# High products ahead of low ones within a slice, and a final norm that is transposed in the last pair, scaled per token at the end

## The chip, the cores and the metric

The kernel runs on one core of a Trainium2 chip. The metric is device time in microseconds for one call. TensorE multiplies (its clock has two levels here, 1.2 and 2.4 GHz; the profile gives the granted share of 2.4), VectorE and ScalarE do elementwise work, GpSimd and SyncE issue transfers. Each engine works through its own instructions in order and waits on semaphores.

## What is computed

One inference step of a two-layer diffusion backbone on 128 context tokens and 128 latent tokens, all float32:

```python
def rms_norm(x, g):
    y = x * rsqrt(mean(x * x, axis=-1) + 1e-6)
    return y * g

for l in range(2):
    h = rms_norm(x, g_attn[l]) * (1 + scale1) + shift1      # modulation: silu(c) @ w_ada + b_ada
    proj = h @ w_in[l]                                      # 2048 -> 3584
    mix = concat(conv_module(...), global_attention(...), windowed_attention(...))
    x = x + gate1 * (mix @ w_out[l])                        # 2048 -> 2048
    h2 = rms_norm(x, g_mlp[l]) * (1 + scale2) + shift2
    x = x + gate2 * (square(relu(h2 @ w_mlp1[l])) @ w_mlp2[l])   # 2048 -> 8192 -> 2048
y = rms_norm(x, g_final)                                    # for both token groups
```

## The kernel before

The residual stream `xT` lies transposed in SBUF: 16 tiles of 128 channels, each with 256 token columns (128 context, 128 latent, `S` = 2 groups). Every weight matrix is cut into pairs of 512 output columns by 2048 rows; `walk` lists the pairs of a layer in order for all engines: in1, in2, in3, out, then four chunks of up and down. There are 43 pairs a layer, 86 in all. The pair of the last four output tiles is written apart from its loop and is called with `last` true.

A product in float32 is made of reduced-precision parts. ScalarE rounds a weight tile to `hi` (`split_hi`, L622), VectorE subtracts it from the raw weights to give `lo` (`split_lo`, L808). The activations are split too and lie side by side: columns 0 to 255 the high part, 256 to 511 the low part. Of the four partial products three are kept: `hi` times all 512 columns (L466), and `lo` times the 256 high ones, added onto columns 256 to 511 of the same bank (L468). ScalarE and VectorE then add both halves of the bank.

TensorE's loop is `pair` (from L447). For each half g of a pair (two banks, j = 0 and 1) it goes through four slices h of four k tiles; a slice waits once for its `lo` and, except in a fresh stage, once for its activations, and for each k it issues, for j = 0 and then j = 1, the high product and the low product. The last product of a slice increments `half_used`, which frees the slice's weight buffers. Weights pass through four `raw` buffers, loaded by SyncE, and four `hi` and `lo` buffers; `split_hi` number o of a pair waits until slice o - 4 is used. In ScalarE's and VectorE's `pair` the splits o = 4g+3 to 4g+6 stand ahead of the drains of half g, so ScalarE works in this order: four splits, the copy of two banks (L667), two squares of the new residual tiles (L678).

After the down pairs the residual is complete. VectorE has added up the squares per channel row in `ssq` (L888). Then comes the final norm, in order: TensorE sums the squares per token (`norm_stats`, L386), ScalarE takes the root (L796), VectorE the reciprocal `tok_rstd` (L1072), TensorE spreads it over all partitions into bank 7 (L390), VectorE multiplies each of 32 tiles by gain and spread value into `yT` (L1076), TensorE transposes them by fours (L612), ScalarE drains each bank into `xtok` (L800), and SyncE stores each drained 128x512 piece (L355), eight stores of 256 KB with rows of 2 KB.

Of the kernel before, what the change touches and what calls it, by code (L numbers as in the profile page):

```python
# [96 lines left out]
def build(nc, t):  # L97
# [77 lines left out]
    yT = place("yT", [P, KT, TOK], f32, act2_at)  # L175
# [50 lines left out]
    out_turned, out_drained, yT_ready = sem("out_turned"), sem("out_drained"), sem("yT_ready")  # L226
# [80 lines left out]
    with block:  # L307
# [3 lines left out]
        def _(sp):  # L311
# [40 lines left out]
            for b in range(8):  # L352
                s, q = b % 2, b // 2
                sp.wait_ge(out_drained, b + 1)
                sp.dma_start(t["y"][s].rearrange("a q d -> (a q) d")[:, q * 512:(q + 1) * 512],  # L355
                             xtok[:, s, q * 512:(q + 1) * 512]).then_inc(y_stored, 16)
            sp.wait_ge(y_stored, 8 * 16)
# [23 lines left out]
        def _(pe):  # L381
            def norm_stats(q):


                for s in range(S):
                    mm = pe.matmul(pb[7][:, s:s + 1], ssq[:, s * P:(s + 1) * P], ones[:, 0:1], start=True, stop=True)  # L386
                mm.then_inc(stat_ready, 1)
                pe.wait_ge(tok_rstd_ready, q + 1)
                for s in range(S):
                    mm = pe.matmul(pb[7][:, TOK + s * P:TOK + (s + 1) * P],  # L390
                                   tok_rstd[:, s:s + 1].to_broadcast([P, P]), ident, start=True, stop=True)
                mm.then_inc(rstd_spread, 1)

# [52 lines left out]
            for l in range(DEPTH):  # L446
                def pair(kind, n, i, c, a, last, l=l):  # L447
                    acts = act2 if kind in ("out", "down") else hs
                    for g in range(2):
# [4 lines left out]
                        for h in range(4):  # L454
                            pe.wait_ge(lo_ready, 8 * n + 4 * g + h + 1)
                            if kind == "down":
                                pe.wait_ge(act2_ready, hidden_base(l, c) + 4 * (h + 1))
                            elif kind != "out" and not fresh:
                                pe.wait_ge(hs_ready, (2 * l + (kind == "up")) * NORM_STEPS + 8 * (h + 1))
                            for k in range(4):  # L460
                                if fresh:
                                    pe.wait_ge(hs_ready, (2 * l + (kind == "up")) * NORM_STEPS + 8 * h + 2 * (k + 1))
                                for j in range(2):
                                    k_ = 4 * h + k
                                    bank = pb[2 * g + j]
                                    pe.matmul(bank[:, :], hi[:, h, k, j * P:(j + 1) * P], acts[:, k_, :],  # L466
                                              start=(k_ == 0), stop=False)
                                    mm = pe.matmul(bank[:, TOK:2 * TOK], lo[:, h, k, j * P:(j + 1) * P],  # L468
                                                   acts[:, k_, 0:TOK], start=False, stop=(k_ == KT - 1))
                            mm.then_inc(half_used, 1)  # L470
                            if a is not None and h == 2:
                                for u in range(2):
                                    ada_unit(*vector_of(kind, i, a, c), a, 4 * quarter(kind, i, a) + 2 * g + u)
                            if kind == "in3" and h % 2 == 1:
                                qk_norms(l, 4 * (i - IN2) + 2 * g + h // 2)
                    if a is not None and quarter(kind, i, a) == 3:
                        vl, vm = vector_of(kind, i, a, c)
                        ada_turn(vl * VECTORS + vm)

# [126 lines left out]
            norm_stats(2 * DEPTH)  # L606
            for b in range(8):
                s, q = b % 2, b // 2
# [8 lines left out]
        def _(act):  # L617
# [33 lines left out]
            for l in range(DEPTH):  # L651
                def pair(kind, n, i, c, a, last, l=l):
                    for g in range(2):
                        if kind == "in3":
                            qk_norms(l, 4 * (i - IN2) + 2 * g)
                        for o in range(4 * g + 3, 4 * g + 7):
                            if not (last and o >= 8):
                                split_hi(n, o)
                        if kind == "in3":
# [9 lines left out]
                        for j in range(2):  # L669
# [4 lines left out]
                            elif kind in ("out", "down"):  # L674
# [4 lines left out]
                                               ACT.Square).then_inc(sq_ready, 1)  # L679

# [113 lines left out]

            act.wait_ge(stat_ready, 2 * DEPTH + 1)
            act.activation(tok_std[:, :], pb[7][:, 0:S], ACT.Sqrt, bias=eps[:, :], scale=1.0 / D).then_inc(std_ready, 1)  # L796
            for b in range(8):
                s, q = b % 2, b // 2
                act.wait_ge(out_turned, b + 1)
                act.activation(xtok[:, s, q * 512:(q + 1) * 512], pb[b % 4][:, :], ACT.Copy).then_inc(out_drained, 1)  # L800
# [3 lines left out]
        def _(dve):  # L804
# [342 lines left out]
```

## Time and profile before

| | us |
|---|---|
| median of 3 runs | 2440.06 (2438.89 to 2440.91) |
| profiled execution, its own time | 2436.85 |
| its span, first to last instruction | 2435.2 |
| mean granted TensorE clock | 0.975 |
| TensorE busy, matmul | 2295.0 (94%) |
| TensorE busy, weight loads | 1826.7 (75%) |
| VectorE busy | 1518.7 (62%) |
| ScalarE busy | 1064.2 (44%) |
| last high-low products | to 2416.2 |
| final norm, transposes and stores | 2419.74 to 2435.2 |

The profile is one execution; it names engine, line, operation and tile of each group of instructions. Matmuls are pipelined: the recorded duration of a product is longer than the distance from one start to the next, and the distance is what a stream costs. A weight load overlaps the product ahead of it.

### The profile page before, as it was taken

What the parts mean: (1) busy time and instruction counts of PE and PEld (TensorE: products, weight loads), DVE (VectorE), ACT (ScalarE), POOL (GpSimd) and SP (SyncE); (2) the same over time, 40 slices, a digit from 0 to 9 for tenths busy, and PEclk for the clock granted to TensorE, in tenths of its full rate; (3) what the DMA queues carried; (4) which work ended last, traced back from release to release, by engine and by line L of the source; (5) the groups of instructions that cost most, each with busy time, mean ns of one, the idle gap of its engine ahead of it and who ended that gap; (6) DMA issues with size and microseconds to landing.
All of it is one profiled execution on the core that took longest, in us unless ns stands there. A gap on an engine that the chain in (4) does not pass through costs nothing.

```text
span 2435.2 us, 36896 instructions
## 1 busy us (share of the span) xinstructions
PE 2295.0 (94%) x13206; PEld 1826.7 (75%) x13206; DVE 1518.7 (62%) x2606; ACT 1064.2 (44%) x1663; POOL 101.6 (4%) x196
## 2 busy tenths in 40 slices
PE   5699879989999999999998997798999999999998
PEld 1277657767887887887786775586788888888886
DVE  0457775575665665565566678767566666666665
ACT  1343334454443443444444342455444545445443
POOL 2000000000000000000000000000000000000000
PEclk9699989999999999999999999999999999999999
DMA  9888645969579669768855885255956555555652
GB/s 386 331 332 300 243 180 211 320 242 324 182 244 319 231 198 314 254 196 294 295 183 204 301 318 214 97 187 189 313 198 196 176 193 186 182 194 176 193 188 87
DMA packets 390556, 570.29 MB, mean 234 GB/s; under 512 B 9604, under 2 KB 364472, under 8 KB 365624
## 3 DMA queue, kind: packets, MB, share of 16 engines
q1 hardware_dynamic: 360504, 365.51, 46.5%
q0 software_dynamic: 27648, 201.34, 20.5%
q10 hardware_dynamic: 2304, 2.10, 0.2%
q8 instruction: 65, 1.06, 0.2%
q14 instruction: 35, 0.29, 0.0%
HBM read 565.76 MB, written 3.15 MB: 234 GB/s over the span
## 4 chain that ended last, share of the span: by engine, by line
PE 86%; DVE 7%; DMA 4%; ACT 2%; issue 1%; POOL 0%; DVEq 0%; ACTq 0%; POOLq 0%
PE bank L466 52%; PE bank L468 26%; PE bank L403 6%; DMA ada<-in_w_ada 4%; DVE hs L1051 1%; DVE ybuf L1043 1%; DVE qrs L938 1%; DVE yconv L901 1%; DVE lo L808 1%; PE bank L483 0%; ACT prob L759 0%; DVE yT L1076 0%; PE bank L421 0%; PE bank L390 0%; PE bank L511 0%
## 5 line engine op out<-in xcount | busy, mean ns | idle before, releaser
L466 PE MATMUL bank<-hs,hi 128*128 128x512 f32 x2944 | 1067.6, 406 | 18.6 <-DVE hs L1051 9.9
L808 DVE TENSOR_TENSOR lo<-raw,hi 128x1024 fp32r<-128x1024 f32 x685 | 816.6, 1222 | 402.2 <-ACT hi L622 401.4
L622 ACT ACTIVATE hi<-raw 128x1024 fp32r<-128x1024 f32 x685 | 706.3, 1054 | 502.7 <-PE bank L468 497.4
L466 PE MATMUL bank<-act,hi 128*128 128x512 f32 x2560 | 908.0, 400 | 5.4 <-DVE act L989 5.4
L468 PE MATMUL bank<-hs,lo 128*128 128x256 f32 x2944 | 830.5, 282 | 0.0
L466 PEld LDWEIGHTS bank<-hs,hi 128*128 128x128 f32 x2944 | 557.9, 189 | 220.4 <-issue 56.4
L468 PE MATMUL bank<-act,lo 128*128 128x256 f32 x2560 | 719.3, 281 | 0.0
L466 PEld LDWEIGHTS bank<-act,hi 128*128 128x128 f32 x2560 | 482.4, 188 | 131.5 <-issue 6.7
L468 PEld LDWEIGHTS bank<-hs,lo 128*128 128x128 f32 x2944 | 560.9, 191 | 2.5 <-issue 2.5
L468 PEld LDWEIGHTS bank<-act,lo 128*128 128x128 f32 x2560 | 484.8, 189 | 0.0
L667 ACT ACTIVATE tmp<-bank 128x256 f32<-128x256 f32 x344 | 113.5, 382 | 443.9 <-PE bank L468 443.9
L863 DVE TENSOR_TENSOR tsum<-bank,tmp 128x256 f32<-128x256 f32 x288 | 121.0, 420 | 237.6 <-ACT tmp L667 237.6
L403 PE MATMUL bank<-ada,cT 128*32 128x512 f32 x1344 | 170.0, 620 | 11.6 <-DMA ada<-in_w_ada 11.6
L367 POOL DMA_DIRECT2D ada<-in_w_ada x160 | 84.4, 528 | 1607.0 <-PE bank L403 1579.6
L678 ACT ACTIVATE thid<-xT 128x256 f32 (+1 forms) x160 | 66.9, 418 | 155.7 <-DVE xT L872 154.7
L872 DVE SCALAR_TENSOR_TENSOR xT<-tsum,mods,xT 128x128 f32 (+1 forms) x320 | 98.3, 348 | 35.5 <-DVE tsum L863 34.2
L403 PEld LDWEIGHTS bank<-ada,cT 128*32 128x32 f32 x1344 | 34.6, 110 | 89.7 <-issue 65.4
L901 DVE SCALAR_TENSOR_TENSOR yconv<-hpad,vecs,yconv 128x256 f32<-128x256 f32 x240 | 96.6, 477 | 0.0
L888 DVE TENSOR_TENSOR ssq<-ssq,thid 128x256 f32<-128x256 f32 x160 | 67.6, 422 | 28.3 <-ACT thid L678 26.2
L672 ACT ACTIVATE act<-thid 128x256 fp32r<-128x256 f32 x128 | 53.5, 418 | 67.1 <-DVE thid L866 67.1
L880 DVE TENSOR_TENSOR act<-thid,act 128x256 fp32r<-128x256 f32 x128 | 53.9, 421 | 9.6 <-ACT act L672 3.8
L866 DVE SCALAR_TENSOR_TENSOR thid<-tsum 128x256 f32<-128x256 f32 x128 | 54.4, 425 | 4.4
(127 smaller groups left out, 712.9 us busy)
## 6 DMA issues: line engine op xcount, KB each, us to landing
raw<-in_w_mlp SPq DMA_DIRECT2D x256, 1024.0 KB, 5.8
ada<-in_w_ada POOLq DMA_DIRECT2D x168, 1024.0 KB, 7.4
raw<-in_w_in SPq DMA_DIRECT2D x56, 1024.0 KB, 5.4
raw<-in_w_out SPq DMA_DIRECT2D x32, 1024.0 KB, 5.3
pre_a<-in_w_ada POOLq DMA_DIRECT2D x16, 1024.0 KB, 18.4
pre_q<-in_w_ada POOLq DMA_DIRECT2D x8, 1024.0 KB, 18.7
xtok<-in_x_prompt SPq DMA_DIRECT2D x1, 1024.0 KB, 14.2
xtok<-in_x_sample SPq DMA_DIRECT2D x1, 1024.0 KB, 32.5
```

What stands on the lines that cost most here:

```text
L367: pool.dma_start(ada[:, k % 2, :], src[:, k, bass.ds(m * D, D)]).then_inc(ada_landed[k % 2], 16)
L403: mm = pe.matmul(ada_ps[32 * q:32 * q + 32, :], cT[:, k, :], unit[:, q * 512:(q + 1) * 512], start=(k == 0), stop=(k == KT - 1))
L466: pe.matmul(bank[:, :], hi[:, h, k, j * P:(j + 1) * P], acts[:, k_, :], start=(k_ == 0), stop=False)
L468: mm = pe.matmul(bank[:, TOK:2 * TOK], lo[:, h, k, j * P:(j + 1) * P], acts[:, k_, 0:TOK], start=False, stop=(k_ == KT - 1))
L622: act.activation(hi[:, o % 4, :, :], raw[:, (o // 2) % 4, 4 * (o % 2):4 * (o % 2) + 4, :], ACT.Copy).then_inc(hi_ready, 1)
L667: act.activation(tmp[:, j, :], pb[2 * g + j][:, TOK:2 * TOK], ACT.Copy)\
L678: act.activation(thid[:, j:j + 1, :], xT[:, bass.ds(4 * i + 2 * g + j, 1), :], ACT.Square).then_inc(sq_ready, 1)
L808: dve.tensor_tensor(lo[:, o % 4, :, :], raw[:, (o // 2) % 4, 4 * (o % 2):4 * (o % 2) + 4, :], hi[:, o % 4, :, :].bitcast(f32), ALU.subtrac ...
L863: dve.tensor_tensor(tsum[:, j, :], bank, tmp[:, j, :], ALU.add).then_inc(bank_freed, 1)
L872: dve.scalar_tensor_tensor(x, tsum[:, j:j + 1, s * P:(s + 1) * P], mods[:, l, bass.ds(gate + 4 * i + 2 * g + j, 1), s], x, ALU.mult, ALU.a ...
L888: dve.tensor_tensor(ssq[:, :], ssq[:, :], thid[:, j, :], ALU.add)\
L901: dve.scalar_tensor_tensor(y, hpad[:, ch, :, bass.ds(tap, P)], vecs[:, l, 1, bass.ds(4 * tap + ch, 1)], y, ALU.mult, ALU.add).then_inc(con ...
```

## The change

**The order in a slice.** The loop over j that issued the high and the low product together is two loops: both high products of a k tile, then both low ones.

**The final norm.** `yT` and its 32 VectorE instructions go. In their place `xg`, the residual times the gain alone, is made by ScalarE, tile by tile. Tiles 0 to 11 are made behind the splits of the last pair's first half, 12 and 13 in its second half, 14 and 15 after it. TensorE transposes tiles 0 to 3, 4 to 7 and 8 to 11 (for both token groups) within the last pair, behind the slices 2, 4 and 6 of its eight, into banks 4 to 7; ScalarE drains them between its splits. After the last pair TensorE sums the squares as before, doesn't spread the reciprocal, and transposes tiles 12 to 15 without waiting for it. Tokens are now on partitions, so the token's factor is a scalar per partition: VectorE scales the first 1024 columns of each token group, ScalarE the other 1024 (512 out of the bank, 512 in place). SyncE makes four stores of 512 KB with rows of 4 KB.

```diff
@@ tensor engine, in pair
-                                for j in range(2):
-                                    k_ = 4 * h + k
-                                    bank = pb[2 * g + j]
-                                    pe.matmul(bank[:, :], hi[:, h, k, j * P:(j + 1) * P], acts[:, k_, :],
+                                k_ = 4 * h + k
+                                for j in range(2):
+                                    pe.matmul(pb[2 * g + j][:, :], hi[:, h, k, j * P:(j + 1) * P], acts[:, k_, :],
                                               start=(k_ == 0), stop=False)
-                                    mm = pe.matmul(bank[:, TOK:2 * TOK], lo[:, h, k, j * P:(j + 1) * P],
+                                for j in range(2):
+                                    mm = pe.matmul(pb[2 * g + j][:, TOK:2 * TOK], lo[:, h, k, j * P:(j + 1) * P],
                                                    acts[:, k_, 0:TOK], start=False, stop=(k_ == KT - 1))
                             mm.then_inc(half_used, 1)
+                            if last and 4 * g + h in (2, 4, 6):
+                                turn_tiles(2 * g + h // 2 - 1)
...
+            def final_turn(q, s, bank):
+                for k in range(4):
+                    mm = pe.transpose(bank[:, k * P:(k + 1) * P], xg[:, 4 * q + k, s * P:(s + 1) * P], ident)
+                mm.then_inc(out_turned, 1)
...
+                def turn_tiles(q):
+
+                    pe.wait_ge(xg_ready, 4 * (q + 1))
+                    if q == 2:
+                        pe.wait_ge(out_drained, 2)
+                    for s in range(S):
+                        final_turn(q, s, pb[4 + (2 * q + s) % 4])
@@ tensor engine, at the end
-            norm_stats(2 * DEPTH)
-            for b in range(8):
-                s, q = b % 2, b // 2
-                pe.wait_ge(yT_ready, 8 * (q + 1))
-                after(pe, out_drained, b - 3)
-                for k in range(4):
-                    mm = pe.transpose(pb[b % 4][:, k * P:(k + 1) * P], yT[:, 4 * q + k, s * P:(s + 1) * P], ident)
-                mm.then_inc(out_turned, 1)
+            pe.wait_ge(out_drained, 6)
+            for s in range(S):
+                mm = pe.matmul(pb[7][:, s:s + 1], ssq[:, s * P:(s + 1) * P], ones[:, 0:1], start=True, stop=True)
+            mm.then_inc(stat_ready, 1)
+            pe.wait_ge(bank_freed, 4 * PAIRS - 2)
+            pe.wait_ge(xg_ready, KT)
+            for s in range(S):
+                final_turn(3, s, pb[s])
@@ scalar engine
                         for o in range(4 * g + 3, 4 * g + 7):
                             if not (last and o >= 8):
                                 split_hi(n, o)
+                            if last:
+                                final_tiles(o - 3)
...
+                def final_tiles(slot):
+
+
+                    if slot < 4:
+                        for k in range(3 * slot, 3 * slot + 3):
+                            gained(k)
+                    elif slot == 4:
+                        drain_tiles(0)
+                    elif slot == 5:
+                        gained(12)
+                        gained(13)
+                        drain_tiles(1)
+                    elif slot == 7:
+                        drain_tiles(2)
+
+                def gained(k):
+                    act.wait_ge(x_updated, 2 * (res_tiles(DEPTH - 1, CHUNKS - 1) + k) + 2)
+                    act.activation(xg[:, k, :], xT[:, k, :], ACT.Copy,
+                                   scale=vecs[:, 0, 2, V_GF + k:V_GF + k + 1]).then_inc(xg_ready, 1)
...
+            for s in range(S):
+                act.wait_ge(out_turned, 7 + s)
+                act.activation(xtok[:, s, 1536:2048], pb[s][:, :], ACT.Copy, scale=tok_rstd[:, s:s + 1])\
+                   .then_inc(y_scaled[1], 1)
+                act.activation(xtok[:, s, 1024:1536], xtok[:, s, 1024:1536], ACT.Copy, scale=tok_rstd[:, s:s + 1])\
+                   .then_inc(y_scaled[1], 1)
@@ vector engine, at the end
-            dve.wait_ge(rstd_spread, 2 * DEPTH + 1)
-            for k in range(KT):
-                for s in range(S):
-                    dve.scalar_tensor_tensor(yT[:, k, s * P:(s + 1) * P], xT[:, k, s * P:(s + 1) * P],
-                                             vecs[:, 0, 2, V_GF + k:V_GF + k + 1], pb[7][:, TOK + s * P:TOK + (s + 1) * P],
-                                             ALU.mult, ALU.mult).then_inc(yT_ready, 1)
+            dve.wait_ge(out_drained, 6)
+            dve.wait_ge(tok_rstd_ready, 2 * DEPTH + 1)
+            for s in range(S):
+                dve.tensor_scalar(xtok[:, s, 0:D // 2], xtok[:, s, 0:D // 2], tok_rstd[:, s:s + 1], None,
+                                  ALU.mult).then_inc(y_scaled[0], 1)
@@ sync engine, at the end
+            for s in range(S):
+                for part in range(2):
+                    cols = slice(part * (D // 2), (part + 1) * (D // 2))
+                    sp.wait_ge(y_scaled[part], (s + 1) * (1 + part))
+                    sp.dma_start(t["y"][s].rearrange("a q d -> (a q) d")[:, cols],
+                                 xtok[:, s, cols]).then_inc(y_stored, 16)
```

## Rows read from the trace of the kernel before

**Rows 1.** The page, chain of work that ended last, by line

```profile
PE bank L466 52%; PE bank L468 26%; PE bank L403 6%; DMA ada<-in_w_ada 4%; DVE hs L1051 1%; DVE ybuf L1043 1%; DVE qrs L938 1%; DVE yconv L901 1%; DVE lo L808 1%; PE bank L483 0%; ACT prob L759 0%; DVE yT L1076 0%; PE bank L421 0%; PE bank L390 0%; PE bank L511 0%
```

**Rows 2.** Stretches: us, PE, PEld, DVE, ACT, POOL (instructions), PEclk, DMA share, GB/s

```profile
2300.00:2400.00 100.00, 100.00 (x568) 86.67 (x567) 64.76 (x102) 49.04 (x72) 0.00 (x0) 1.00 0.54 174
```

**Rows 3.** Timeline of the last pair: start us, us, engine line op out<-in

```profile
2413.88 0.28 PE L468 MATMUL bank<-act,lo 128*128 128x256 f32 x1
2413.88 0.19 PEld L466 LDWEIGHTS bank<-act,hi 128*128 128x128 f32 x1
2413.99 0.40 PE L466 MATMUL bank<-act,hi 128*128 128x512 f32 x1
2414.22 0.28 PE L468 MATMUL bank<-act,lo 128*128 128x256 f32 x1
2414.34 0.40 PE L466 MATMUL bank<-act,hi 128*128 128x512 f32 x1
```

**Rows 4.** Timeline of TensorE after a long wait, and its granted clock there

```profile
290.26 0.63 PE L466 MATMUL bank<-hs,hi 128*128 128x512 f32 x1
290.69 0.41 PE L468 MATMUL bank<-hs,lo 128*128 128x256 f32 x1
290.90 0.60 PE L466 MATMUL bank<-hs,hi 128*128 128x512 f32 x1
...
290.00:291.00 1.00, 1.00 (x5) 0.85 (x4) 1.00 (x3) 0.00 (x0) 0.00 (x0) 0.50 0.00 0
```

**Rows 5.** Timeline, weight loads under 8-column products

```profile
605.56 0.98 PEld L421 LDWEIGHTS bank<-cst,rows 128*128 128x128 f32 x8
```

**Rows 6.** Timeline of TensorE: transposes at the start; products after modulation work

```profile
56.04 3.69 PE L440 MATMUL bank<-cst,xtok 128*128 128x128 f32 x32
...
919.01 0.50 PE L466 MATMUL bank<-hs,hi 128*128 128x512 f32 x1
919.34 0.28 PE L468 MATMUL bank<-hs,lo 128*128 128x256 f32 x1
```

**Rows 7.** Timeline of the end

```profile
2419.74 0.61 PE L386 MATMUL bank<-ones,ssq 128*128 128x1 f32 x4 [3.47 <-DVE ssq L888]
2420.39 0.26 ACT L796 ACTIVATE tok_std<-bank,eps 128x2 f32<-128x2 f32 x1 [1.16 <-PE bank L386]
2420.68 0.17 DVE L1072 RECIPROCAL tok_rstd<-tok_std 128x2 f32<-128x2 f32 x1 [0.99 <-ACT tok_std L796]
...
2421.87 8.35 DVE L1076 SCALAR_TENSOR_TENSOR yT<-xT,vecs,bank 128x128 f32<-128x128 f32 x32 [1.02 <-PE bank L390]
...
2425.22 0.60 ACT L800 ACTIVATE xtok<-bank 128x512 f32<-128x512 f32 x1 [4.58 <-PE bank L612]
2425.85 0.36 SPq L355 DMA_DIRECT2D out_y_prompt<-xtok  x1
```

**Rows 8.** Busy time by stretches at the end (last columns DMA share, GB/s)

```profile
2426.00:2427.00 1.00, 0.90 (x5) 0.86 (x5) 1.00 (x5) 0.60 (x1) 0.00 (x0) 0.50 0.28 111
2427.00:2428.00 1.00, 1.00 (x6) 0.71 (x4) 1.00 (x5) 0.60 (x1) 0.00 (x0) 0.50 0.84 326
...
2430.00:2431.00 1.00, 0.72 (x7) 0.73 (x8) 0.22 (x1) 0.03 (x1) 0.00 (x0) 1.00 0.99 320
...
2426.00:2434.10 8.10, 4.20 (x25) 3.28 (x24) 4.22 (x17) 3.96 (x7) 0.00 (x0) 0.87 0.76 259
```

**Rows 9.** Timeline of ScalarE in the last pair

```profile
2397.28 3.20 ACT L622 ACTIVATE hi<-raw 128x1024 fp32r<-128x1024 f32 x3
...
2418.81 0.42 ACT L678 ACTIVATE thid<-xT 128x256 f32<-128x256 f32 x1 [0.57 <-DVE xT L872]
```

**Rows 10.** Groups by shape: line engine op out<-in xcount | busy us, mean ns

```profile
L808 DVE TENSOR_TENSOR lo<-raw,hi 128x1024 fp32r<-128x1024 f32 x685 | 816.6, 1222 | 402.2 <-ACT hi L622 401.4
...
L1020 DVE TENSOR_SCALAR prob<-prob,rinv 128x256 f32<-128x256 f32 x24 | 8.3, 347 | 0.0
...
L1020 DVE TENSOR_SCALAR prob<-prob,rinv 128x128 f32<-128x128 f32 x24 | 6.9, 286 | 0.8
```

More of the change, by code:

```diff
@@ L174, in build @@
     nmean = place("nmean", [P, TOK], f32, act2_at + 29696)
-    yT = place("yT", [P, KT, TOK], f32, act2_at)
+    xg = place("xg", [P, KT, TOK], f32, hs_at + 16384)
     xsq = place("xsq", [P, KT, TOK], f32, hs_at + 16384)
@@ L225, in build @@
         sem("probT_ps"), sem("probT_ready"), sem("out_ready"), sem("out_hi"))
-    out_turned, out_drained, yT_ready = sem("out_turned"), sem("out_drained"), sem("yT_ready")
+    out_turned, out_drained, xg_ready = sem("out_turned"), sem("out_drained"), sem("xg_ready")
+    y_scaled = [sem("y_scaled_by_vector"), sem("y_scaled_by_scalar")]
     def walk(eng, layer, pair, stage):
@@ L351, in _ @@
                 walk(sp, l, load_pair, lambda name, c: None)
-            for b in range(8):
-                s, q = b % 2, b // 2
[L354 to L357, printed above, removed]
+            for s in range(S):
[4 more added lines that the diff above has]
+                                 xtok[:, s, cols]).then_inc(y_stored, 16)
+            sp.wait_ge(y_stored, 4 * 16)
             sp.wait_ge(kv_stored, DEPTH * 4 * 16)
@@ L605, in _ @@
             pe.wait_ge(ssq_steps, ssq_base(DEPTH, -1))
-            norm_stats(2 * DEPTH)
-            for b in range(8):
-                s, q = b % 2, b // 2
-                pe.wait_ge(yT_ready, 8 * (q + 1))
-                after(pe, out_drained, b - 3)
-                for k in range(4):
-                    mm = pe.transpose(pb[b % 4][:, k * P:(k + 1) * P], yT[:, 4 * q + k, s * P:(s + 1) * P], ident)
-                mm.then_inc(out_turned, 1)
+            pe.wait_ge(out_drained, 6)
[6 more added lines that the diff above has]
+                final_turn(3, s, pb[s])
         @block.scalar
@@ L679, in pair, with drain_tiles @@
                                                ACT.Square).then_inc(sq_ready, 1)
+                def final_tiles(slot):
[14 more added lines that the diff above has]
+                                   scale=vecs[:, 0, 2, V_GF + k:V_GF + k + 1]).then_inc(xg_ready, 1)
+                def drain_tiles(q):
+                    for s in range(S):
+                        act.wait_ge(out_turned, 2 * q + s + 1)
+                        act.activation(xtok[:, s, q * 512:(q + 1) * 512], pb[4 + (2 * q + s) % 4][:, :], ACT.Copy)\
+                           .then_inc(out_drained, 1)
                 def squares(l, q):
@@ L793, in _ @@
                 walk(act, l, pair, stage)
+            for k in range(14, KT):
+                act.activation(xg[:, k, :], xT[:, k, :], ACT.Copy,
+                               scale=vecs[:, 0, 2, V_GF + k:V_GF + k + 1]).then_inc(xg_ready, 1)
             act.wait_ge(stat_ready, 2 * DEPTH + 1)
             act.activation(tok_std[:, :], pb[7][:, 0:S], ACT.Sqrt, bias=eps[:, :], scale=1.0 / D).then_inc(std_ready, 1)
[L797 to L800, printed above, removed]
+            act.wait_ge(out_drained, 6)
+            act.wait_ge(tok_rstd_ready, 2 * DEPTH + 1)
+            for s in range(S):
[4 more added lines that the diff above has]
+                   .then_inc(y_scaled[1], 1)
         @block.vector
@@ L1072, in _ @@
             dve.reciprocal(tok_rstd[:, :], tok_std[:, :]).then_inc(tok_rstd_ready, 1)
-            dve.wait_ge(rstd_spread, 2 * DEPTH + 1)
-            for k in range(KT):
-                for s in range(S):
-                    dve.scalar_tensor_tensor(yT[:, k, s * P:(s + 1) * P], xT[:, k, s * P:(s + 1) * P],
-                                             vecs[:, 0, 2, V_GF + k:V_GF + k + 1], pb[7][:, TOK + s * P:TOK + (s + 1) * P],
-                                             ALU.mult, ALU.mult).then_inc(yT_ready, 1)
+            dve.wait_ge(out_drained, 6)
+            dve.wait_ge(tok_rstd_ready, 2 * DEPTH + 1)
+            for s in range(S):
+                dve.tensor_scalar(xtok[:, s, 0:D // 2], xtok[:, s, 0:D // 2], tok_rstd[:, s:s + 1], None,
+                                  ALU.mult).then_inc(y_scaled[0], 1)
 def head(e):
```

## Prediction

> **What bounds the kernel now.** I read the chain of work that ended last first: two lines of TensorE, the high products (L466) and the low products (L468), hold 52% and 26% of it [rows 1]. Then the busy time by stretches: from 600 to 2400 us TensorE is busy for 100.00 of 100 us in 13 of 18 stretches (the others hold the norms and the attention of layer 1), and in each of the six without modulation work 568 products show, two of them cut by the edges [rows 2]. So the middle is a pure stream of products, and no wait ends last in it. Its law is in the timeline: a low product starts at 2413.88, the high one at 2413.99, the next low one at 2414.22, the next high one at 2414.34 [rows 3]. 100 us hold 283 high-low pairs, so a pair takes 100 / 283 = 353.4 ns, and the chain's 52% to 26% splits it into about 236 ns for the 512-column product and 118 ns for the 256-column one [rows 1]. The code has 86 pairs of banks x 64 = 5504 such product pairs, 5504 x 0.3534 = 1945 us: 1 ns a pair is 5.5 us.
>
> Last the end of the trace [rows 7]: a serial stretch from the statistics' matmul (2419.74) over the square root, the reciprocal and the spread to 32 VectorE instructions of the final norm (2421.87, 8.35 us together), with transposes, drains and eight stores following in their wake; the span ends at 2435.2.
>
> I make the sums against the profiled execution: its span is 2435.2 us and its own time 2436.85. The median of the runs is 2440.06, 3.2 us more; I carry the difference over unchanged.
>
> **Part 1: the order of products.** Each slice of the k loop now issues high(j=0), high(j=1), low(j=0), low(j=1) instead of high, low, high, low. Nothing is removed or added: same 11008 products, same weight loads, same waits (they stand ahead of the slice or of the k step), same last instruction of a slice. So it can pay only through the hand-over from product to product, and the question is what the 353.4 ns are made of. 768 columns at 2.4 GHz are 320 ns; 33.4 ns are excess. Three readings:
>
> (a) The excess is a rate. 236 to 118 is 2 to 1, as 512 columns to 256: both products are stretched by the same 10%. The hand-over from high to low stays in a bank, that from low to high changes it, and both carry the same share. In the stretch where the granted clock was 0.50 (the 1.2 GHz level) the starts are 290.26, 290.69, 290.90: 640 ns a pair, exactly 768 columns at 1.2 GHz, no excess [rows 4]. A limit on how fast columns of this type stream (at some 2.17 columns a ns) explains all three and doesn't know the order. Price of the change: 0.
>
> (b) The excess sits in hand-overs (a low product accumulating onto the columns that the high one has just written). Then 1.2 GHz hides it too, since all distances double in time. That is rival A.
>
> (c) The load of the next weights sets the pace under the short product. The load starts with the product before it (2413.88 in both rows) [rows 3]. Its recorded 0.19 us is longer than 118 ns, but loads overlap: eight of them under 8-column products take 0.98 us, (0.98 - 0.19) / 7 = 113 ns apart [rows 5]. 113 is under 118, with 5 ns to spare. The new order puts two short products in a row, so two loads without a long cover between them; at 113 ns each still has its own 118. Price 0, else rival B.
>
> I take (a), the row that shows both sizes and both clocks. Bounds for what I can't see: a gain up to the whole excess, 33.4 x 5504 = 184 us; a loss up to the recorded load time, where each pair would hold one long and one short product of 236 and 190: 72 x 5504 = 396 us.
>
> The Trainium skill, page "TensorE: Matmul & The Clock Gate", section "Back-to-back issue gap", puts the isolated gap of a warm product at its columns over 2.4 GHz plus 2.5 ns, which would be 216 and 109, 325 ns a pair. The rows here say 353.4; by the rows the change of order gives 0, by the page there are 28.4 ns a pair to be had if the old order is what withholds them, 156 us and a time of 2282. The trace as it stands is against the page's gap, and rival A is where it would come true.
>
> **Part 2: twelve tiles of the final norm move into the last pair.** Three times eight transposes now stand between slices of the last pair, where TensorE is the bound and nothing hides them. Before, these cost TensorE time in the shadow of VectorE. 32 such transposes took 3.69 us at the start of the kernel, 115 ns each; eight are 0.92 [rows 6]. Coming back costs something: after a block of other matmuls, high at 919.01 to low at 919.34 is 0.33 instead of 0.24, 0.09 more [rows 6]. 3 x (0.92 + 0.09) = **+3.0 us** on the path. Bounds: 3 x (8 x 0.110) = 2.6, and 3.8 if each block also drains once (0.27).
>
> ScalarE gets 14 scalings there and six drains. One 128x256 instruction took 0.42 us, a split 3.20 / 3 = 1.07 [rows 9], a drain 0.60 [rows 7]. The last pair starts 64 x 0.3534 = 22.6 us before 2416.2, at 2393.6. The splits o=3 to 5 begin late, at 2397.28, behind the squares of the pair before [rows 9]. With three scalings behind each: split 3 to 2398.35, scalings 0 to 2 to 2399.6, split 4 to 2400.7, scaling 3 to 2401.1. TensorE asks for tiles 0 to 3 after its third slice, 2393.6 + 3 x 2.83 = 2402.1: 1.0 us of margin. Low halves go on: split 4 is followed by its subtraction of 1.22 us [rows 10], ready at 2401.9, needed by slice 4 at 2405.8; split 5, 2403.0 to 2404.2 against 2409; split 6, 2405.3 to 2406.5 against 2411; split 7 comes after the drains of bank group 0 and the squares, 2410.6 to 2411.8 against 2415. The drain of the first two tiles follows at 2411.8, and TensorE needs it after slice 6 at 2415. So ScalarE's queue hides all 20 instructions, price 0. If that cover is gone TensorE waits for what is late; that is in rival C. The wait for out_drained and xg_ready on TensorE has the rest of the last pair queued behind it.
>
> Scalings 14 and 15 follow the last squares (2418.81 + 0.42, then 0.84 us, 2420.1) [rows 9] and are ahead of the square root, which waits until 2420.39 anyway: hidden, 0.3 us to spare. VectorE loses 32 instructions and gets two.
>
> **Part 3: the end.** Times here without the 3.0 us. Up to the reciprocal nothing changes: 2420.68 + 0.17 = 2420.86 [rows 7]. The spread and the 8.35 us of the final norm go. In their place VectorE scales 128x1024 from SBUF: 128 columns took 286 ns, 256 took 347, so 0.48 ns a column and 286 + 896 x 0.48 = 0.71 us (bounds 0.71 and the 1.22 of a 128x1024 tensor_tensor) [rows 10]. The first half token row is ready at 2420.90 + 0.71 = 2421.61, the next VectorE half at about 2422.3. ScalarE does four 512-column instructions, 0.60 us alone, about 0.48 apart: ready at 2422.0 and 2423.1; its first waits for the last transposes, which start behind the statistics' matmul at 2420.3 and end by 2421.0. Four stores of 512 KB are issued by SyncE from 2421.65 on, one about every 0.4 us.
>
> What is late next is the store itself. Before, issue at 2425.85, data from 2426.66 (111 GB/s in 2426 to 2427 is a third of a microsecond at the 326 of the next one): 0.81 us. Then 8.1 us at 259 GB/s and 0.76 share, 2.10 MB in all, that is 340 GB/s at full share; then almost nothing moves for the 1.1 us to the end [rows 8]. The DMA rows were paced by the norm before; now all 2.10 MB are wanted within 1.5 us, so they take 2.10 / 0.340 = 6.2 us (bounds from single microseconds: 326 / 0.84 = 388, 5.4 us; 320 / 0.99 = 323, 6.5 us). I take 340, the whole of the same stores, though each row is 4 KB now and not 2. End: 2421.65 + 0.81 + 6.2 + 1.1 = 2429.8 against 2435.2: **-5.4 us**.
>
> The Trainium skill, page "DMA: Bandwidth & Descriptors", section "Anatomy of one DMA", fits the moving of data at 436 bytes a ns; by it the 2.10 MB would take 4.8 us and the end come 1.4 us earlier still. No row here reaches that rate.
>
> Sum: +3.0 - 5.4 = -2.4 us, 2432.8 for the span and 2440.06 - 2.4 = **2437.7** for the median. Bounds of the sum: best 2.6 - 5.4 - 0.8 = -3.6; worst 3.8 - 5.4 + 0.3 + 0.5 = -0.8. With 1 us of scatter on the median its own range is 2435.3 to 2440.5. A measurement can tell this kernel from no change at 0.2%, 4.9 us; the forecast is inside that.
>
> **The rivals.**
>
> A, the hand-over: consecutive products in one bank cost the excess, and alternating banks gives it back. For: the excess is there at one clock only. Against: low to high changes banks already and has its 10% all the same. The long product could fall to its 512 columns at 2.4 GHz, 213 ns, the short one to the 113 ns of its load, 326 together: 27.4 x 5504 = 151 us, 2287; half of it 2362.
>
> B, two loads in a row (slower): under low, low, high each load must be done in 118 ns with no long product to catch up under. It decides where a load needs more than 118 ns; 113 was measured under other weights. At 125 ns, 7 ns a short product and one short product a pair: 7 x 5504 = 38 us, 2476. Against: in the old order too each load under a short product had only its 118, since none starts before the product ahead of it.
>
> C, the last pair stalls: if ScalarE reaches scaling 3 later than 2402.1, TensorE waits there, and the splits behind slip too. Decides at 1.0 us of lateness; it makes the kernel slower than before once the waits exceed 2.4 us. At 5 us: 2443.
>
> D, a small effect of the order, under 2 ns a pair either way (a bubble at slice ends, the spare 5 ns used up in part): up to 11 us, 2427 to 2449.
>
> **How the numbers follow.** Forecast 0.62 (0.58 within 0.2%, 0.04 faster since scatter can carry it over), A 0.12, B 0.08, C 0.04 (half within, half slower), D 0.14 (0.07 faster, 0.02 within, 0.05 slower). Faster 0.04 + 0.12 + 0.07 = 0.23; within 0.58 + 0.02 + 0.02 = 0.62; slower 0.08 + 0.02 + 0.05 = 0.15. The forecast and C and D together are 0.80, so the range is theirs: 2427 to 2448.
>
> **What would show it.** Right: 567 or 568 products in 100 us as before; starts 236, 236, 118, 118 ns apart; three blocks of about 1 us of transposes in the last 26 us with no wait ahead of them; data leaving for 6.2 us in one piece behind the first store, and 1.1 us of nothing. Wrong: any other count of products in 100 us, which outweighs all the rest; in the order of starts a short hand-over of about 109 for A, over 118 after a low product for B; a wait of TensorE on xg or xtok in the last pair for C; a store rate far from 340 GB/s moves the end by at most 1 us.

## The result and the profile after

The changed kernel takes **2412.72 us** (median of 4 runs, 2408.40 to 2412.95) against 2439.55 before (4 runs): ratio **0.9885**, 95% interval 0.9868 to 0.9902, 27 us or 1.1% less. The forecast was 2437.7 with a range of 2427 to 2448: most of its chance lay on no change beyond 0.2%, and the measured time is below the range.

Busy time by stretches of the kernel after, three of the stretches of 100 us and the whole as the page has it (columns as in [rows 2]):

```profile
span 2411.2 us, 36873 instructions
PE 2271.0 (94%) x13202; PEld 1823.9 (76%) x13202; DVE 1512.6 (63%) x2576; ACT 1069.7 (44%) x1681; POOL 101.6 (4%) x196
...
700.00:800.00 100.00, 100.00 (x611) 76.80 (x611) 53.44 (x75) 40.92 (x60) 8.45 (x16) 1.00 0.93 323
2000.00:2100.00 100.00, 100.00 (x577) 87.26 (x576) 66.84 (x100) 50.17 (x73) 0.00 (x0) 1.00 0.60 189
2200.00:2300.00 100.00, 100.00 (x576) 87.26 (x576) 65.97 (x95) 50.67 (x74) 0.00 (x0) 1.00 0.62 189
```

TensorE is full as before, but 100 us hold 576 or 577 products where they held 568 [rows 2]. By the starts of 1216 pairs of high and low product in layer 1, a pair takes 348.3 ns; the same reading of the kernel before gives 353.3, so it is 5.0 ns less. This is the row that the prediction named as the one that outweighs the others. The end, from the start of the last low product to the end of the span, took 19.2 us before (2415.99 to 2435.2) and takes 12.9 us now (2398.33 to 2411.2). The timeline of the kernel after, with the first and the last block of transposes within the last pair and the end:

```profile
2380.41 1.29 ACT L717 ACTIVATE xg<-xT,vecs 128x256 f32<-128x256 f32 x3
...
2381.89 1.04 PE L398 MATMUL bank<-cst,xg 128*128 128x128 f32 x8
...
2394.55 0.40 PE L475 MATMUL bank<-act,lo 128*128 128x256 f32 x2
...
2394.79 1.04 PE L398 MATMUL bank<-cst,xg 128*128 128x128 f32 x8
...
2395.58 0.70 PE L472 MATMUL bank<-act,hi 128*128 128x512 f32 x2
...
2402.08 1.01 PE L625 MATMUL bank<-ones,ssq 128*128 128x1 f32 x4 [3.47 <-DVE ssq L940]
...
2403.43 0.17 DVE L1124 RECIPROCAL tok_rstd<-tok_std 128x2 f32<-128x2 f32 x1 [1.40 <-ACT tok_std L844]
2403.70 1.42 DVE L1128 TENSOR_SCALAR xtok<-xtok,tok_rstd 128x1024 f32<-128x1024 f32 x2
...
2404.48 1.36 SPq L357 DMA_DIRECT2D out_y_prompt<-xtok  x2
...
2405.94 0.72 ACT L851 ACTIVATE xtok<-xtok,tok_rstd 128x512 f32<-128x512 f32 x1
```

and the stores in its stretches, where [rows 8] had 326 and 320 GB/s:

```profile
2404.00:2405.00 1.00, 0.91 (x5) 0.50 (x3) 1.00 (x2) 0.83 (x2) 0.00 (x0) 0.50 0.00 0
2405.00:2406.00 1.00, 0.00 (x0) 0.00 (x0) 0.12 (x1) 1.00 (x3) 0.00 (x0) 0.50 0.70 291
2406.00:2410.00 4.00, 0.00 (x0) 0.00 (x0) 0.00 (x0) 0.65 (x2) 0.00 (x0) 0.50 1.02 418
```

The reader is to see three things. No wait stands ahead of the blocks of transposes; the fourth scaling was done 1.0 us before TensorE came to the first block. The new path behind the reciprocal (2403.60) is short: 0.88 us to the first store's issue. And the stores run as one piece, at 418 GB/s from 2406 to 2410.

### The profile page after: what moved, and what is told of

The parts are those of the page before. It is cut to its first block, busy times and chain, and to the rows that moved or that the text cites. A ratio compares the mean times of both kernels' runs of the same rounds, so it can differ in the third digit from the quotient of the medians.

```text
span 2411.2 us, 36873 instructions
## 1 busy us (share of the span) xinstructions
PE 2271.0 (94%) x13202; PEld 1823.9 (76%) x13202; DVE 1512.6 (63%) x2576; ACT 1069.7 (44%) x1681; POOL 101.6 (4%) x196
## 4 chain that ended last, share of the span: by engine, by line
PE 86%; DVE 7%; DMA 4%; ACT 2%; issue 1%; POOL 0%; ACTq 0%; DVEq 0%; POOLq 0%
PE bank L472 53%; PE bank L475 26%; PE bank L410 6%; DMA ada<-in_w_ada 4%; DVE hs L1103 1%; DVE ybuf L1095 1%; DVE qrs L990 1%; DVE yconv L953 1%; DVE lo L860 1%; PE bank L500 1%; ACT prob L804 0%; PE bank L428 0%; PE bank L528 0%; DVE zq L996 0%; PE bank L392 0%
## 5 line engine op out<-in xcount | busy, mean ns | idle before, releaser
L472 PE MATMUL bank<-hs,hi 128*128 128x512 f32 x2944 | 946.8, 403 | 18.9 <-DVE hs L1103 10.1
L472 PE MATMUL bank<-act,hi 128*128 128x512 f32 x2560 | 809.5, 398 | 5.4 <-DVE act L1041 5.4
L475 PE MATMUL bank<-hs,lo 128*128 128x256 f32 x2944 | 582.3, 279 | 0.0
L472 PEld LDWEIGHTS bank<-hs,hi 128*128 128x128 f32 x2944 | 452.6, 190 | 86.4 <-issue 60.5
L475 PE MATMUL bank<-act,lo 128*128 128x256 f32 x2560 | 504.9, 279 | 0.0
L472 PEld LDWEIGHTS bank<-act,hi 128*128 128x128 f32 x2560 | 391.9, 190 | 12.4 <-issue 6.7
L940 DVE TENSOR_TENSOR ssq<-ssq,thid 128x256 f32<-128x256 f32 x160 | 67.8, 423 | 28.3 <-ACT thid L697 25.8
```

What stands on the lines that cost most here:

```text
L472: pe.matmul(pb[2 * g + j][:, :], hi[:, h, k, j * P:(j + 1) * P], acts[:, k_, :], start=(k_ == 0), stop=False)
L475: mm = pe.matmul(pb[2 * g + j][:, TOK:2 * TOK], lo[:, h, k, j * P:(j + 1) * P], acts[:, k_, 0:TOK], start=False, stop=(k_ == KT - 1))
L940: dve.tensor_tensor(ssq[:, :], ssq[:, :], thid[:, j, :], ALU.add)\
```

## The experiments

All are compared with the kernel before. A kernel that ran once stands beside one run of the kernel before (2436.76, 2436.84 or 2438.36 us); there the distances between starts carry the argument and not the time. The distances in nanoseconds below are differences of neighbouring starts in the traces; 100-us counts of the view by stretches stand beside them.

**Which part brings the time.** `order_only` is the kernel before with the new loop alone, `tail_only` the changed kernel with the old loop:

```diff
-                                for j in range(2):
-                                    ... high(k, j); low(k, j)
+                                for j in range(2):
+                                    ... high(k, j)
+                                for j in range(2):
+                                    ... low(k, j)
```

> The kernel before with the new order of products alone. In the trace of after a high-low pair takes 348.4 ns where it took 353.4. If the order does that by itself: 348.4 ns again, 5504 x 5.0 = 27 us less than before, about 2412 to 2416. If the new end were worth more than its -2.4 us and the order less, the pair would still tell: 353.4 would mean that something else in the change moved it.

Measured: 2414.9 us against 2438.61, ratio 0.9904 (0.9887 to 0.9921), 24 us less.

> The changed kernel with the old order of products. By the prediction's sum for parts 2 and 3: -2.4 us, 2437.2 against a median before of 2439.6. By the trace of after (end of products to end of span 12.9 us where it was 19.1, less three blocks of transposes of 0.9 us): -3.5 us. A pair stays at 353.4 ns.

Measured: 2434.43 us, ratio 0.9982 (0.9972 to 0.9991), 4.2 us less. The same stretch of each, `order_only` first:

```profile
2000.00:2100.00 100.00, 100.00 (x576) 87.30 (x575) 66.55 (x99) 49.51 (x73) 0.00 (x0) 1.00 0.60 189
```

```profile
2000.00:2100.00 100.00, 100.00 (x568) 86.67 (x567) 65.75 (x102) 48.72 (x72) 0.00 (x0) 1.00 0.59 188
```

The parts add up (0.9904 x 0.9982 = 0.9886), and nearly all is the order of the products: 576 with it, 568 without.

**Why the order matters: size changes or banks?** The new order does two things at once: sizes come in twos (512, 512, 256, 256), and each product writes another bank than the one ahead of it. `eight` groups sizes further; `same_bank` groups sizes by two but stays in a bank for eight products; `alt_banks` changes the bank at all but two of sixteen products and lets sizes alternate (but for the first slice of a bank group).

```diff
 eight
-    for k: high(k, 0), high(k, 1), low(k, 0), low(k, 1)
+    for k: high(k, 0), high(k, 1)
+    for k: low(k, 0), low(k, 1)
 same_bank
+    for j: for k in (0, 2): high(k, j), high(k + 1, j), low(k, j), low(k + 1, j)
 alt_banks
+    for k: high(k, 0), low(k, 1)
+    for k: high(k, 1), low(k, 0)      # h == 0 has high(0, 1) second, which opens its bank
```

> The changed kernel, but a slice issues all its eight high products and then all its eight low ones (two changes of size in sixteen products, where after has eight and before sixteen). Theory S, a change between 512 and 256 columns costs 5 ns each (before two a pair, after one): 0.25 a pair, 344.6 ns, 20 us less than after, 2392. Theory K, two products in a row into one bank cost 5 ns: banks change at each product here as in after, 348.4 ns, same time as after.

Measured: 2413.78 us, ratio 0.9900 (0.9883 to 0.9917), 349.2 ns a pair. Neither theory's number: 4.6 ns over S, 0.8 over K.

> The changed kernel, but a slice does for j = 0 and then j = 1: high, high, low, low of two neighbouring k tiles, so that sizes come in twos as in after but the bank stays for eight products. Theory S: 348.4 ns a pair, the time of after. Theory K: each product but one in eight follows one in its own bank, twice as often as in before: 353.4 ns at least, up to 358; 27 to 55 us more than after.

Measured: 2412.90 us, ratio 0.9895 (0.9879 to 0.9912), 348.3 ns a pair, and start for start the distances of the kernel after. K falls here: products in one bank, one after the other, cost nothing.

> The changed kernel, but sizes alternate at each product as in before while the bank changes at each product as in after (high of j = 0 with low of j = 1 through the slice, then high of j = 1 with low of j = 0). Theory S: 353.4 ns a pair. Theory K: 348.4.

Measured: 2423.55 us in one run, 350.3 ns a pair. Between S and K, which neither allows. The rows, in the order `eight`, `same_bank`, `alt_banks`:

```profile
2000.00:2100.00 100.00, 100.00 (x576) 88.02 (x575) 66.22 (x99) 50.33 (x74) 0.00 (x0) 1.00 0.60 189
```

```profile
2000.00:2100.00 100.00, 100.00 (x576) 87.25 (x575) 66.17 (x100) 49.66 (x72) 0.00 (x0) 1.00 0.59 189
```

```profile
2000.00:2100.00 100.00, 100.00 (x573) 87.17 (x572) 65.57 (x101) 49.63 (x72) 0.00 (x0) 1.00 0.60 190
```

**One size only.** In both wide kernels the low product takes 512 columns.

```diff
-    low:  pe.matmul(bank[:, TOK:2 * TOK], lo[...], acts[:, k_, 0:TOK], ...)
+    low:  pe.matmul(bank[:, :], lo[...], acts[:, k_, :], ...)
```

> The changed kernel in the old order, but the low product takes all 512 activation columns too (it adds the fourth partial product, low by low), so that there is one size only. Theory S: no change of size, so the distance of two 512-column products is the same as in wide_new. Theory K: 2.5 ns a product more than wide_new, since every second product follows one in its bank.

> The same in the new order. It gives the distance of 512-column products in a pure stream: 233 ns if the 20 ns over 512 columns at 2.4 GHz are a rate or a cost of each product, 216 or less if sizes next to each other make them. A kernel about 5504 x 118 = 650 us longer.

Measured: 2981.25 and 2977.89 us, one run each. In the plain stretches of both every product starts 226.7 ns after the one ahead, none otherwise, and 100 us hold the same number (`wide_old`, then `wide_new`):

```profile
2600.00:2700.00 100.00, 100.00 (x443) 82.84 (x442) 52.04 (x81) 38.09 (x56) 0.00 (x0) 1.00 0.46 144
```

```profile
2600.00:2700.00 100.00, 100.00 (x443) 82.79 (x442) 51.77 (x80) 38.42 (x54) 0.00 (x0) 1.00 0.46 146
```

So bank order is nothing here either, and a 512-column product in a pure stream takes 226.7 ns: not the 233 nor the 216 that I had put up, and 10 less than the 236 it takes in the kernel before. With `eight`, whose long runs settle, the pattern is plain. Its slice, start to start:

```
high 233 236 228 233 231 227 227 227   low 113 119 120 120 120 120 120 120
```

Settled, 512 columns take 226.7 = 213.3 + 13.3 ns and 256 columns take 120.0 = 106.7 + 13.3. The overhead is the same for both sizes, not the same share. After a change of size five long products pay 27.4 ns together before they settle, and the first two short ones win 7.5: 20 ns over the eight pairs of a slice, and 226.7 + 120.0 + 2.5 is the 349.2 of `eight`. All this is at the 2.4 GHz level. Where the kernel after runs with its clock at 0.50 (1560 to 1564 us), the products start 427 and 213 ns apart, 640 a pair as in [rows 4]: there is neither an overhead nor an effect of the order.

**What the old order does.** Read start by start, the old order doesn't have one pace. Both lines are from the kernel before, the same loop:

```
at 2100 us:  low 117 high 241 low 120 high 236 low 113 high 233, and again    3 pairs 1060 ns, 353.3 a pair
at 1610 us:  low 118 high 231 low 112 high 233, and again                     2 pairs  693.3 ns on average, 346.7 a pair
```

The view by stretches had it too (kernel before; from 1600 to 1660 are out pairs of layer 1):

```profile
2000.00:2030.00 30.00, 30.00 (x172) 26.02 (x171) 20.03 (x32) 15.77 (x22) 0.00 (x0) 1.00 0.51 169
1600.00:1630.00 30.00, 30.00 (x175) 26.21 (x174) 20.06 (x32) 14.17 (x21) 0.00 (x0) 1.00 0.65 210
1630.00:1660.00 30.00, 30.00 (x175) 26.25 (x174) 20.27 (x32) 15.58 (x22) 0.00 (x0) 1.00 0.55 172
```

The fast rhythm takes exactly what the two sizes take in settled streams of their own, 226.7 + 120.0 = 346.7 ns, and the slow one 6.7 ns more. (The recorded expectations say 347.1 for the fast one, a little too much: 498 products in a row give 346.7.) The order of the products alone doesn't fix which one a stage gets: `tail_only` has the same products in the same order up to the last pair, yet its out pairs of layer 1 run at 353.4, with 172 products from 1600 to 1630 us and not 175.

Hence theory P: a stream of alternating sizes runs in one of two steady rhythms, and whatever stood ahead of it picks one. It explains `alt_banks`: behind the first slice of a bank group its slices run entirely in one or entirely in the other. Two kernels test it. They put back the old loop, with a quad, the four products of one k tile, in the new order at a few places:

```diff
 nudge_half
+    twos = h == 0 and k == 0
 nudge_slice
+    twos = k == 0
```

> The changed kernel with the old order of products everywhere but in the first k tile of each bank group, one quad in 64 products, which keeps high, high, low, low. Theory S (each change of size has its price): 353.4 ns a pair less 0.6, since one in sixteen quads has two changes fewer. Theory P (a stream of alternating sizes runs in one of two steady rhythms, 353.3 or 347.1 ns a pair, and what stands ahead of it selects which; the kernel before shows 347 in its out pairs of layer 1 and 353 elsewhere): stretches between two quads are at 353.3 or at 347.1 and nothing between, with some at 347.1 in the stages where before has 353.3.

> The same with the quad at the start of each slice, one in four. Theory S: 353.4 - 0.25 x 5 = 352.1 ns a pair. Theory P: the three quads behind it in each slice are in one of the two rhythms, so a pair is anywhere from 347 to 353 and can be below after's 348.4.

Measured: `nudge_half` 2424.97, `nudge_slice` 2413.46 us, one run each; 349.9 and 349.6 ns a pair. The starts of `nudge_half` around two quads, 11 us apart (the quads in brackets; a number is the time from the start of that product to the next start):

```
... h240 l120 h236 l114 h232 l118 h240 l120 h236 l114 [h232 h236 l116 l112] h233 l117 h231 l113 h232 l118 h230 l113 ...
... h231 l113 h232 l118 h230 l113 h232 l118 h231 l112 [h233 h231 l113 l119] h233 l118 h241 l120 h236 l113 h232 l118 ...
```

One quad takes the stream from the slow rhythm to the fast one, and the next takes it back; in between, for 60 products, it stays. In all 38 bank groups of the plain stretch read here (layer 1, 1960 to 2385 us) the two take turns, 353.4 and 346.7. In `nudge_slice` they take turns from slice to slice. S falls: the sizes alternate in both rhythms. The row of `nudge_half`, half fast and half slow:

```profile
2000.00:2100.00 100.00, 100.00 (x574) 87.06 (x573) 66.46 (x101) 49.07 (x72) 0.00 (x0) 1.00 0.60 189
```

The new order is then a stream of nothing but such quads, in which the two kinds of the lines above follow each other (233 236 116 113, 232 231 113 119: 696.7 ns each on average, 348.3 a pair), and it never enters the slow rhythm.

**Using it.** `guided` and `guided2` keep the old loop and place quads by rule, so that the stream is in the fast rhythm as often as may be:

```diff
+    if last or kind == "in3":
+        twos = True
+    elif a is not None:
+        twos = h == 3 and k == 0
+        # guided2 only: the first up pair of chunks 1 to 3
+        if kind == "up" and i == 0 and not (isinstance(c, int) and c == 0):
+            twos = twos or (g, h, k) == (0, 0, 0)
+    elif kind == "out":
+        twos = False
+    else:
+        twos = (g, h, k) in ((0, 0, 0), (1, 3, 3))
```

> The changed kernel with the old order of products, and single high, high, low, low quads put where they should move the stream from the 353.3 rhythm to the 347.1 one: behind each block of modulation products (the fourth slice of the bank group), and at the first and last k tile of each up or down pair without such a block; the in3 pairs and the last pair keep after's order. Theory P: most stretches at 347.1, a pair on average 347.3 to 348, 3 to 6 us less than after where the state at the entry of a pair is the slow one; where it is the fast one, 353.3 in those pairs. Theory S: 353.3 less a few tenths, 25 us more than after.

Measured: 2407.25 us in one run. The down pairs and most others run at 346.8 ns a pair, the twelve up pairs (of the kernel's 86, with 64 high-low pairs each) of layer 0's later chunks at 353.1: there the quad behind the modulation block was one too many.

> guided with one quad more, at the first k tile of the first up pair of chunks 1 to 3. In guided the up pairs of layer 0 in those chunks ran at 353.3, since the modulation block left the stream in the fast rhythm and the quad behind it moved it to the slow one. Theory P: the added quad turns that round, those 12 pairs of 64 products go to 347.1, 768 x 6.2 = 4.8 us less than guided's 2407.3: 2402 to 2404, ratio to before about 0.986, against 0.9885 to 0.990 of the kernels with after's order. If the modulation block resets the rhythm whatever stands ahead of it, they stay at 353.3 and the time at 2407. Theory S: no effect.

Measured: 2404.69 us (2402.26 to 2409.22), ratio **0.9866** (0.9849 to 0.9882). Those twelve pairs now run at 346.8, so the switch works as forecast. The same stretch of `guided`, then of `guided2`:

```profile
700.00:800.00 100.00, 100.00 (x603) 77.33 (x600) 53.63 (x79) 41.36 (x62) 8.46 (x16) 1.00 0.92 326
```

```profile
700.00:800.00 100.00, 100.00 (x615) 76.48 (x614) 53.97 (x76) 41.34 (x61) 8.46 (x16) 1.00 0.94 326
```

The time of the profiled run is nearly `guided`'s all the same (2406.52 against 2407.25): nine other pairs that no added quad touches, layer 0's out 1 to 3 and first up 1 to 3 and layer 1's out 1 to 3 (counted from 0), run at 353.1 to 353.4 where `guided` had 346.7 to 346.9, 3.7 us in all. Which rhythm follows a wait isn't fixed by the program, and the rule of quads doesn't fix it either.

Its median is 8 us under that of the kernel after, which had 611 products from 700 to 800 us; the intervals of the two ratios overlap a little. So it is shown that `guided2` beats the kernel before, and likely that it beats the kernel after.

**The rate of the stores.** `rows_2k` issues each of the four last stores as two of half the row.

```diff
+    for q in (2 * part, 2 * part + 1):
+        cols = slice(q * 512, (q + 1) * 512)
```

> The changed kernel with each of the four last stores issued as two of 256 KB with rows of 2 KB. The trace of after moves 414 GB/s at full share, the trace of before 340. If the row size makes the rate: 340, the last data 1.1 us later. If it was a busy neighbour or a queue that ran empty in before: 414 again, no later than 0.2 us.

Measured: 2411.86 us in one run. From the reciprocal's end to the end of the span it takes 9.2 us (2400.97 to 2410.2), the kernel after 7.6 (2403.60 to 2411.2). Its stretches:

```profile
2402.00:2403.00 1.00, 0.27 (x2) 0.00 (x0) 0.48 (x1) 1.00 (x3) 0.00 (x0) 0.50 0.28 111
2403.00:2408.00 5.00, 0.00 (x0) 0.00 (x0) 0.00 (x0) 1.02 (x2) 0.00 (x0) 0.50 1.07 331
```

331 GB/s at full share with rows of 2 KB, 418 with rows of 4 KB, and from the last low product to the end of the span 14.5 us and not 12.9. So the rate belongs to the way the bytes are cut, and a busy neighbour or an empty queue isn't needed to explain the kernel before. In the traces each row is a packet: a row of 4 KB takes 159 ns, always; a row of 2 KB takes 84 ns in the median, but the slowest tenth takes 150 and more. `rows_2k` halves the rows and doubles the number of stores at once, as the kernel before has it, so rows and count of stores aren't told apart. The time of the whole says nothing on it, since 1.6 us are less than the scatter between runs.

## Why the prediction was wrong, point by point

**The order of products, step (a), failed.** It took the excess of 33.4 ns a pair for a rate that the order can't touch, because 236 to 118 is 2 to 1, and so priced the change of order at 0; it was worth 5.0 ns a pair, 27.5 us. The 236 and 118 were means over a rhythm of three pairs (241, 236, 233 and 120, 113, 117), and their ratio is an accident: `eight` and the wide kernels show 13.3 ns a product for either size, 26.7 a pair, and 6.7 more that belong to the slow rhythm. That a hand-over has a price that depends on what came before it, I had only as (b), tied to banks. `same_bank` and the wide kernels refute banks, so rival A was wrong in its mechanism and, at 151 us, in its size. Rival D had the right kind of effect, a small one of the order, but at most 2 ns a pair, where 5 were measured. The low clock's 640 ns, taken as the sign of a rate, are 640 in both orders.

The Trainium skill, "TensorE: Matmul & The Clock Gate", section "Back-to-back issue gap", gives an isolated gap of columns over 2.4 GHz plus 2.5 ns, 216 for 512 columns. No stream here reaches it; the nearest is 226.7.

**The row that would have told was there.** I read the middle as one pace from stretches of 100 us and put those with less than 100 us busy aside as norms and attention. [Rows 2] shows a slow stretch only. The two stretches of 30 us from 1600 to 1660 show 175 products each where the slow rhythm has 172, with the same loop and the same operand shapes. A stream whose pace differs between stages without a wait has an unexplained term, and that term was the forecast's uncertainty: 6.7 ns a pair, 37 us, not the 2 ns that rival D allowed.

**Rival B** (loads in a row) had the wrong sign: the two short products of a quad take 116 and 113 or 113 and 119 ns, 115 on average, where the old order has 117. In longer rows they settle at 120.0 (`eight`), 2 over the forecast's 118; no run tells whether that is the load or the product.

**Rival C** didn't happen. The forecast's account of ScalarE holds to a tenth: scaling 3 was forecast 1.0 us ahead of TensorE; it was done at 2380.41 + 0.49 = 2380.90, and the first block starts at 2381.89.

**Part 2, the blocks of transposes**: forecast +3.0 us, at its lower bound of 2.6. From the last low product ahead of a block (2394.67) to the next high one (2395.58) it is 0.91 for 0.12, and that one takes 0.31 for 0.23: 0.87 a block, 2.6 in all.

**Part 3, the end**: forecast -5.4, found 12.9 for 19.2, -6.3 us. The terms: first issue 0.88 us behind the reciprocal (forecast 0.79); issue to first data 0.82 (0.81); VectorE's 128x1024 at 0.71 each (0.71); the data 5.1 us for 2.10 MB, first packet to last (6.2); from there to the end of the span 0.8 (1.1). The transfer was the mis-sized term: I took the rate of 2 KB rows, 340, for 4 KB rows, which give 418, outside my bounds of 323 to 388. The Trainium skill's page "DMA: Bandwidth & Descriptors", section "Anatomy of one DMA", has 436 bytes a ns, fitted on transfers that GpSimd issues. For these stores, which SyncE issues, it was nearer than the row. What the transfer gave was partly taken back: the statistics' matmul and what follows took 1.52 us to the reciprocal's end where it had been 1.12, because the granted clock was at 0.50 there (the 1.2 GHz level) and not at 1.00; in `tail_only`, with the clock at 1.00 in that place, it is 1.11 again. Sum for parts 2 and 3 by the traces +2.6 - 6.3 = -3.7 for the kernel after and +2.6 - 6.7 = -4.1 for `tail_only`, which measured -4.2 (-2.2 to -6.8). Forecast -2.4: right in mechanism and nearly in size.

**Where the whole gain went.** 5504 pairs x 5.0 = 27.5 us, less what three places hold back. The out pairs of layer 1 already ran at 346.7 in the profiled run and now run at 348.3. Behind each block of modulation products the first four pairs gain nothing (1.51 us before, 1.52 after, the restart included). And out of attention the clock came up later; 29 us from the start of that stage in the kernel before, then in the kernel after:

```profile
1571.00:1600.00 29.00, 29.00 (x159) 25.25 (x159) 16.46 (x27) 13.02 (x18) 0.00 (x0) 0.94 0.44 145
```

```profile
1559.00:1588.00 29.00, 28.89 (x151) 25.10 (x152) 15.54 (x26) 12.29 (x20) 0.00 (x0) 0.90 0.45 145
```

The first out pair took 23.9 us and now 24.9, that of layer 0 28.3 and now 29.0; the mean granted clock of the profiled runs is 0.975 and 0.965. From the first high product to the last low one the profiled runs took 2309.1 and 2291.5 us, 17.6 less with 2.6 us of transposes added, so the order brought 20.2 us there; with the end's 6.3 and less the transposes that makes the 23.9 us between the two profiled runs. By the medians the order alone brings 24 us and the whole 27.

## What to carry to other kernels

Before a stream is called uniform, count its instructions in equal stretches of every stage that keeps the engine full, not in one, and look at single distances, not at a mean: here two paces of one loop meant a term that the order could move. Products of two sizes cost as much mixed as apart in one rhythm (346.7 ns a pair) and 6.7 ns more in the other, so the gain comes from which rhythm the stream locks into: try two or three orders and read the distance in each stage. An order that never enters the slow rhythm gives a sure 5.0 ns; chasing the last 1.6 ns works only as far as the rhythm at the entry of each stage is known. A rate taken from one transfer holds only for one cut like it: 340 GB/s in rows of 2 KB became 418 in rows of 4 KB.

## What the runs showed of the hardware

- A product of reduced-precision float32 with its own weight load takes its columns at 2.4 GHz plus 13.3 ns in a settled stream of one size: 226.7 ns for 512 columns (`wide_old`, `wide_new`, `eight`), 120.0 for 256 (`eight`). At the 1.2 GHz level it takes its columns and nothing more, 427 and 213 ns (kernel after, 1560 to 1564 us). Which bank it writes makes no difference (`wide_old` and `wide_new`, `same_bank` and after).
- Alternating 512 and 256 columns, the same instructions run at 353.3 or at 346.7 ns a pair for as long as nothing interrupts them; the fast rhythm held for 498 products in a row in layer 1's out pairs. Four products in another order switch from one to the other (`nudge_half`, `nudge_slice`, `guided2`). Which one follows a wait can differ with the same products (layer 1's out pairs in the kernel before and in `tail_only`). That loads of weights and streams of columns meet in a fixed phase would fit; no run here shows the cause, and it stays open.
- Stores from SBUF moved 331 GB/s in rows of 2 KB (eight stores, `rows_2k`) and 418 in rows of 4 KB (four stores, kernel after) with all queues full.
- Where the clock comes up after a pause differs from trace to trace: the first out pair of layer 1 took 23.9 us before and 24.9 after (granted clock 0.94 and 0.90 over 29 us), and the lower clock at the end of the kernel after cost 0.4 us. It doesn't explain the scatter between runs: `order_only` took 2413.45 us at a mean clock of 0.967 and 2414.95 at 0.974.
